# Two transformer blocks in one kernel: in the second expert layer, each expert's down projection is moved behind the next expert's gate and up, and the residual sum and the stores are done per token tile

## The chip, the core and the metric

The kernel runs on 1 core of a Trainium2 chip. The metric is the device time of one execution in microseconds (us), lower is better. Before the change it is 1803.22 us, the median of 3 runs.

The engines are named as the profile names them: PE is TensorE (matmuls; PEld is its weight load), DVE is VectorE, ACT is ScalarE, POOL is GpSimd, SP is SyncE, which here only issues DMAs. SPq is SP's own instruction queue.

## The reference, cut to what matters

Two blocks over 256 tokens of width 1024, all in float32: the first ends in a layer of 32 experts (top 4), the second in a layer of 32 experts (top 2 of one of 4 groups of 8). The change is in the second expert layer, which is the last thing that the program computes:

```python
x = x + mixed @ w_out[l]                                   # residual of the second block
hn = rms_norm_2(x, norm2_w[l]).reshape(B * S, D)
moe = hierarchical_moe(hn, ..., w_gate_experts[l], w_up_experts[l], w_down_experts[l])
x = x + moe.reshape(B, S, D)
```

Each token goes to two experts e. For its row t, an expert computes `silu(t @ w_gate[e]) * (t @ w_up[e])`, of width 512, and multiplies this by `w_down[e]`, back to width 1024. The outputs are weighted by the gates and added up. Each of the three matrices of an expert is 1024 x 512 or 512 x 1024 in float32, 2 MB.

## The kernel before, in words

The tokens lie as two tiles of 128 partitions (TT = 2) in `h`, which holds the residual. `experts(k)` is written once for each engine; k = 0 is the first layer, k = 1 the second. The kernel gives each expert 32 rows (CAP2) in the second layer. Experts with more tokens would be run again from a list afterwards; in these inputs the list is empty.

**The ring.** Weights stream through `ring`, six slots of 2 MB. In the second layer an expert uses three: gate, up and down. Even experts use slots 0 to 2, odd ones slots 3 to 5. SP issues the loads in the order gate, up, down, expert after expert, from one queue. Before each load (L358) it waits for the slot to be free (`free[s]`), and every later load waits behind it. PE raises `free[s]` at the last matmul that reads the slot. I call the loads g0, u0, d0, g1, and so on. The first six (L347) need only slots that the dense part has left; g2 is the first that needs a slot that an expert has left.

**One expert on PE** is made of these steps:

- `gate_up` (L1660): 128 matmuls recorded, 64 for gate, then 64 for up, into bank 4. It waits for `picked` from DVE and for the two loads.
- `gather_rows` of the next expert (L1612): 16 matmuls that pick its rows out of `h`, by the one-hot matrix that DVE's `choose` wrote. ACT copies the rows (L603, `leave_rows`), PE turns them (`turn_rows`, L1621), and DVE's `gather` writes `picked` (L1011).
- `hid_turn` (L1677) turns the hidden values that DVE's `activate` wrote after ACT's sigmoid (L586); ACT copies them (L595, `leave_hid`).
- `down` (L1687): 32 matmuls into bank 5, which wait for that copy. ACT copies the result to `y` (L599, `leave_y`).
- `back_turn` (L1668) turns the gate matrix that DVE's `gate` wrote; ACT copies it (L590, `leave_back`).
- `scatter` (L1715): 16 matmuls that add `y` to the running sum of all experts in banks 0 to 3.

Before the change PE does, for expert p: `gate_up(p)`, `scatter(p-1)`, `back_turn(p)`, `gather_rows(p+1)`, `hid_turn(p)`, `turn_rows(p+1)`, `down(p)`. The down matmuls of an expert so stand ahead of the gate and up matmuls of the next.

**Around the loop.** Banks 0 to 3 are begun by `fill`. Four matmuls of the identity with `h` (L1589, two records each) put the residual into them while DVE chooses the experts, and one more follows behind the rank matmuls (L1595 to L1599). At the end, DVE (L1212) and ACT (L677) copy two column quarters each from banks 0 to 3 into `h`, and SP (L389) issues four stores of 256 KB, one for each quarter.

Of the kernel before, what the change touches and what calls it, by code (L numbers as in the profile page):

```python
# [26 lines left out]
ALU = mybir.AluOpType  # L27
# [29 lines left out]
def two_blocks(nc, w, out):  # L57
# [11 lines left out]
    with ctx:  # L69
# [241 lines left out]
        def _(sp):  # L311
# [74 lines left out]
            rows_out = out[0].rearrange("(a p) n -> p a n", p=P)  # L386
            for b, who, n in ((2, "d2_copied", 17), (0, "moe_out", 5), (3, "d2_copied", 18), (1, "moe_out", 6)):
                sp.wait_ge(sem(who), n)
                sp.dma_start(rows_out[:, :, T * b:T * (b + 1)], h[:, :, T * b:T * (b + 1)]).then_inc(sem("stored"), 16)  # L389
            sp.wait_ge(sem("stored"), 16 * 4)  # L390
# [85 lines left out]
        def _(act):  # L476
# [86 lines left out]
            def experts(k, ready):  # L563
# [84 lines left out]
                else:  # L648
                    def chained(p, n, s0, ahead=True):
                        sigmoid(q, p, n, s0)  # L650
                        leave_back(q, p)
                        if ahead:
                            leave_rows(q, p + 1)
                        leave_hid(q, p)
                        leave_y(q, p, n, s0)

                    chained(0, 0, 0)
                    with act.Fori(0, E // 2 - 1) as n:
                        chained(2 * n + 1, n, 3)
                        chained(2 * n + 2, n + 1, 0)  # L660
                    chained(E - 1, E // 2 - 1, 3, False)
                    after(act, k, q, "pe", "scattered", E - 1)
                act.wait_ge(sem("list"), k + 1)
                n = act.value_load(lst[0:1, 0:1], min_val=0, max_val=NLIST)
                with act.If(n > 0):
                    with act.Fori(0, n) as p:
# [6 lines left out]
                        if k == 1:  # L673
                            after(act, k, q, "pe", "scattered", p)
                if k == 1:
                    for b in range(2, 4):
                        act.copy(h[:, :, T * b:T * (b + 1)], bank(b).rearrange("p (a n) -> p a n", a=TT)).then_inc(sem("d2_copied"), 1)  # L677
# [79 lines left out]
        def _(dve):  # L757
# [167 lines left out]
            def experts(k):  # L925
# [256 lines left out]
                else:  # L1182
                    def chained(p, n, s0, ahead=True):
                        gate(q, p, p, p)
                        if ahead:
                            choose(q, p + 1)
                        activate(q, p, n, s0)
                        if ahead:
                            gather(q, p + 1)

                    chained(0, 0, 0)
                    with dve.Fori(0, E // 2 - 1) as n:
                        chained(2 * n + 1, n, 3)
                        chained(2 * n + 2, n + 1, 0)
                    chained(E - 1, E // 2 - 1, 3, False)
# [14 lines left out]
                if k == 1:  # L1210
                    for b in range(2):
                        dve.tensor_copy(h[:, :, T * b:T * (b + 1)], bank(b).rearrange("p (a n) -> p a n", a=TT))\  # L1212
                            .then_inc(sem("moe_out"), 1)
# [215 lines left out]
        def _(pe):  # L1429
# [133 lines left out]
            def experts(k):  # L1563
# [18 lines left out]
                def fill(n):  # L1582

                    for b in range(n):
                        by_tile = bank(b % 4).rearrange("p (a n) -> p a n", a=TT)
                        if k == 0:
                            pe.matmul(by_tile, nothing[:, 0:P], nothing[:, None, :].broadcast_to([P, TT, T]), start=True, stop=True)
                        else:
                            pe.matmul(by_tile, ident[:, :], h[:, :, T * (b % 4):T * (b % 4 + 1)], start=True, stop=True)  # L1589

                fill((10, 4)[k])
# [140 lines left out]
                fill((2, 1)[k])  # L1732
# [7 lines left out]
                fill((2, 0)[k])  # L1740
                turn_rows(q, 0)
                fill((2, 0)[k])
# [147 lines left out]
                else:  # L1890

                    def chained(p, n, s0, prev, ahead=True):
                        gate_up(q, p, *main(n, s0))
                        if prev is not None:
# [288 lines left out]
```

## Time and profile before

| what | value |
|---|---|
| median of 3 runs | 1803.22 us (1802.41 to 1804.89) |
| the profiled execution, its own time | 1802.41 us |
| its span, first to last instruction | 1800.7 us |
| PE busy, all of the span | 1709.6 us (95%) |
| DVE, ACT busy | 389.8 us (22%), 246.5 us (14%) |
| granted TensorE clock, mean | 0.999 |
| read from HBM | 653.62 MB, 364 GB/s over the span |

How to read it: the profiled execution's own time is 1.7 us above its span, and 0.8 us below the median. The busy shares are means over stages with different limits. The second expert layer is the stretch from about 1340 us to the end. In the chain of work that ended last, PE has 66% of the whole span and DMA 31%; of the latter, the load of `w_up_experts` has 17% of the span and that of the first layer's `w_up` 14%.

### The profile page before, as it was taken

To read this page: it belongs to the slowest core of one execution; us is meant where nothing else is said; L and a number is where in the kernel's file an instruction comes from. 1 tells how busy PE (TensorE), PEld (TensorE's weight loads), DVE (VectorE), ACT (ScalarE), POOL (GpSimd) and SP (SyncE) were. 2 spreads that over 40 slices of the span, in tenths; PEclk is the share of its full clock that TensorE was granted. 3 is DMA by queue.
4 is the path that set the end of the run, shared out by engine and by line. 5 is a ranking of instruction groups with operands and counts; after the bars stand their busy time and mean duration, and the time that the engine had idled before them with its cause. 6 is when DMAs were issued, how large, how long until landed. Compare 5 with 4: busy or idle time off the path is not lost.

```text
span 1800.7 us, 28719 instructions
## 1 busy us (share of the span) xinstructions
PE 1709.6 (95%) x12156; PEld 765.7 (43%) x12156; DVE 389.8 (22%) x943; ACT 246.5 (14%) x529; POOL 28.1 (2%) x107
## 2 busy tenths in 40 slices
PE   8999999999999999999999999999999988888887
PEld 4543333333333333333332335656446655554454
DVE  3542111121212112122121222342331111111111
ACT  2311111111211101001000011130111111111111
POOL 3020000000000000000000000000000000000000
PEclk9999999999999999999999999999999999999999
DMA  9549999999999997999999995431259999999997
GB/s 312 213 164 430 428 428 428 428 429 428 428 429 428 428 427 318 428 428 429 428 428 429 427 401 206 138 119 47 97 227 428 428 429 428 428 429 427 430 428 322
DMA packets 73526, 655.24 MB, mean 364 GB/s; under 512 B 13216, under 2 KB 16048, under 8 KB 36240
## 3 DMA queue, kind: packets, MB, share of 16 engines
q1 hardware_dynamic: 70736, 651.91, 87.1%
q0 software_dynamic: 528, 1.98, 0.4%
q10 hardware_dynamic: 2224, 0.79, 0.2%
q8 instruction: 29, 0.48, 0.1%
q14 instruction: 9, 0.07, 0.0%
HBM read 653.62 MB, written 1.05 MB: 364 GB/s over the span
## 4 chain that ended last, share of the span: by engine, by line
PE 66%; DMA 31%; DVE 1%; ACT 0%; issue 0%; SPq 0%; ACTq 0%; DVEq 0%
PE ps L1627 28%; DMA ring<-in_w_up_experts 17%; DMA ring<-in_w_up 14%; PE ps L1930 6%; PE ps L1660 6%; PE ps L1990 6%; PE ps L1451 3%; PE ps L1612 3%; PE ps L1709 2%; PE ps L1519 2%; PE ps L1636 1%; PE ps L1621 1%; PE ps L1773 1%; PE ps L1675 1%; PE ps L1687 1%; PE ps L2055 1%
## 5 line engine op out<-in xcount | busy, mean ns | idle before, releaser
L1627 PE MATMUL ps<-ring,Z 128*64 128x512 f32 x3072 | 678.2, 595 | 13.4 <-DMA ring<-in_w_up 12.8
L1627 PEld LDWEIGHTS ps<-ring,Z 128*64 128x64 f32 x3072 | 213.6, 137 | 449.6 <-issue 415.1
L1660 PE MATMUL ps<-ring,Z 128*32 128x128 f32 x4096 | 246.4, 408 | 37.4 <-DMA ring<-in_w_up_experts 24.6
L1660 PEld LDWEIGHTS ps<-ring,Z 128*32 128x32 f32 x4096 | 153.1, 126 | 128.3 <-DMA ring<-in_w_up_experts 36.8
L1990 PE MATMUL ps<-ring,xT 128*128 128x512 f32 (+1 forms) x256 | 105.7, 567 | 0.0
L1612 PE MATMUL ps<-h,Z 128*32 128x256 f32 (+1 forms) x776 | 99.8, 468 | 0.3 <-DVE Z L997 0.3
L1027 DVE TENSOR_SCALAR Z<-ps 128x512 f32<-128x512 f32 x32 | 22.1, 692 | 355.8 <-PE ps L1627 355.8
L1039 DVE TENSOR_TENSOR Z<-Z,ps 128x128 f32<-128x128 f32 x32 | 9.2, 288 | 304.6 <-ACT Z L586 304.6
L599 ACT COPY Z<-ps 128x256 f32<-128x256 f32 (+1 forms) x63 | 30.1, 478 | 303.6 <-PE ps L1627 229.6
L1029 DVE TENSOR_SCALAR Z<-ps 128x512 f32<-128x512 f32 x32 | 22.1, 692 | 227.7 <-PE ps L1627 227.7
L1990 PEld LDWEIGHTS ps<-ring,xT 128*128 128x128 f32 x256 | 47.6, 190 | 48.9 <-issue 48.2
L590 ACT COPY Z<-ps 128x256 f32<-128x256 f32 x64 | 23.8, 373 | 317.2 <-PE ps L1668 317.1
L1709 PE MATMUL ps<-Z 64*128 64x512 f32 x256 | 63.6, 615 | 0.8 <-ACT Z L599 0.8
L1687 PE MATMUL ps<-ring,Z 128*32 128x256 f32 x1024 | 61.9, 382 | 0.4 <-ACT Z L595 0.4
L1451 PE MATMUL ps<-ring,xT 128*128 128x512 f32 x128 | 57.3, 606 | 2.7 <-DMA ring<-in_w_in 2.7
L1011 DVE TENSOR_TENSOR Z<-ps,gcol 128x512 f32<-128x512 f32 (+1 forms) x65 | 36.4, 560 | 99.2 <-PE ps L1621 99.1
L1930 PE MATMUL ps<-ring,xT 128*128 128x512 f32 x128 | 56.1, 594 | 1.5 <-DVE xT L1226 0.8
L583 ACT ACTIVATE Z<-Z 128x512 f32<-128x512 f32 x32 | 20.2, 632 | 244.4 <-DVE Z L1027 244.4
L1019 DVE TENSOR_SCALAR Z<-iota,Z 128x128 f32<-128x128 f32 x128 | 38.5, 343 | 42.7 <-issue 41.3
L586 ACT ACTIVATE Z<-ps 128x128 f32<-128x128 f32 x32 | 8.9, 278 | 270.7 <-PE ps L1660 270.7
L1612 PEld LDWEIGHTS ps<-h,Z 128*32 128x32 f32 (+1 forms) x776 | 29.3, 117 | 38.0 <-issue 29.8
L1709 PEld LDWEIGHTS ps<-Z 64*128 64x128 f32 x256 | 22.1, 186 | 41.5 <-issue 41.5
(421 smaller groups left out, 1167.4 us busy)
## 6 DMA issues: line engine op xcount, KB each, us to landing
ring<-in_w_gate SPq DMA_DIRECT2D x64, 2048.0 KB, 18.6
ring<-in_w_up SPq DMA_DIRECT2D x64, 2048.0 KB, 21.6
ring<-in_w_down SPq DMA_DIRECT2D x64, 2048.0 KB, 18.7
ring<-in_w_gate_experts SPq DMA_DIRECT2D x32, 2048.0 KB, 25.3
ring<-in_w_up_experts SPq DMA_DIRECT2D x32, 2048.0 KB, 25.4
ring<-in_w_down_experts SPq DMA_DIRECT2D x32, 2048.0 KB, 24.9
ring<-in_w_in SPq DMA_DIRECT2D x12, 2048.0 KB, 12.4
ring<-in_w_out SPq DMA_DIRECT2D x4, 2048.0 KB, 19.7
```

Of the source, the lines that this page charges most:

```text
L599: act.copy(y[:, 0:(512, 256)[k]], bank((7, 5)[k])[:, 0:(512, 256)[k]]).then_inc(done_by(q, "act", "y"), 1)
L1011: tt(picked[:, 0:DC * CAPS[k]].rearrange("p (c j s) -> p c j s", **by_chunk), bank(6)[:, 0:DC * CAPS[k]].rearrange("p (c j s) -> p c j s", ...
L1019: ts(gated[:, a].rearrange("p (j s) -> p j s", s=CAPS[k]), iota[:, None, 0:CAPS[k]].broadcast_to([P, P // CAPS[k], CAPS[k]]), rank[:, a, d ...
L1451: last = pe.matmul(bank(j % 2), xT[:, c, a * P:(a + 1) * P], slot(u, DC, 512)[:, c, :], start=c == 0, stop=c == DC - 1)
L1519: last = pe.matmul(bank((4, 5, 0, 1)[b]), xT[:, c, a * P:(a + 1) * P], slot(4 + n, DC, 512)[:, c, :], start=c == 4, stop=c == 3)
L1612: last = pe.matmul(bank(6)[n * j:n * (j + 1), 0:P * c].rearrange("p (q c) -> p q c", c=c), one_hot[:, a, 0:n], h[:, a, :].rearrange("p (q ...
L1627: last = pe.matmul(dst[CAP * j:CAP * (j + 1)], lhsT, rhs(j), start=start, stop=True, skip_group_check=True)
L1660: last = pe.matmul(bank(4)[CAP2 * t:CAP2 * (t + 1), P * s:P * (s + 1)], picked[:, chunk * CAP2:(chunk + 1) * CAP2], v[:, c, t:512:4], star ...
L1687: last = pe.matmul(bank(5)[CAP2 * t:CAP2 * (t + 1), 0:T], hid[:, CAP2 * j:CAP2 * (j + 1)], v[:, j, T * t:T * (t + 1)], start=j == 0, stop= ...
L1709: last = pe.matmul(bank(2 * a + j), back[CAP * j:CAP * (j + 1), a * P:(a + 1) * P], y[CAP * j:CAP * (j + 1), :], start=False, stop=True, s ...
L1930: last = pe.matmul(dst, lhs(c), rhs(c), start=c == 0, stop=c == nc_ - 1)
L1990: last = pe.matmul(bank(i % 2)[:, 0:n], tile(a)(c), v[:, c, :], start=c == 0, stop=c == DC - 1)
```

## The change

In the second expert layer (k = 1; the first is left as it is) the loops of PE, ACT and DVE are written anew as `overlapped`:

- PE now does, for expert p: `gate_up(p)`, `gather_rows(p+1)`, `down(p-1)`, `turn_rows(p+1)`, `hid_turn(p)`, `scatter(p-1)`, `back_turn(p)`. `down(E-1)` and `scatter(E-1)` follow behind the loop. ACT and DVE take their steps in the order that goes with this.
- The `ahead` flag is gone: the last expert too gathers and turns rows for a next one. Nothing uses them.
- The residual no longer goes through the fills. `fill` is now matmuls of bfloat16 zeros in both layers, in the second layer 16 ahead of the choice (before: 4 of `h`), then 3, 1 and 1 (before: 1, 0 and 0).
- At the end DVE alone adds banks 0 to 3 to `h`, one instruction of 128 x 1024 for each token tile, and SP stores each tile as one DMA of 512 KB. ACT's two copies are gone.
- ACT's and DVE's waits for `scattered` are changed to fit.

```diff
--- before.py
+++ after.py
@@ -383,11 +383,10 @@
             last_use = [max(x[1] for x in middle[s::SLOTS]) for s in range(SLOTS)]
             experts(1, lambda s: sp.wait_ge(sem("dense2"), last_use[s]))
 
-            rows_out = out[0].rearrange("(a p) n -> p a n", p=P)
-            for b, who, n in ((2, "d2_copied", 17), (0, "moe_out", 5), (3, "d2_copied", 18), (1, "moe_out", 6)):
-                sp.wait_ge(sem(who), n)
-                sp.dma_start(rows_out[:, :, T * b:T * (b + 1)], h[:, :, T * b:T * (b + 1)]).then_inc(sem("stored"), 16)
-            sp.wait_ge(sem("stored"), 16 * 4)
+            for a in range(TT):
+                sp.wait_ge(sem("moe_out"), 4 + a + 1)
+                sp.dma_start(out[0, a * P:(a + 1) * P, :], h[:, a, :]).then_inc(sem("stored"), 16)
+            sp.wait_ge(sem("stored"), 16 * TT)
 
 
         @block.gpsimd
@@ -646,20 +645,20 @@
                     with act.Fori(EXTRA_AT + 1, E) as p:
                         chained(p)
                 else:
-                    def chained(p, n, s0, ahead=True):
+                    def overlapped(p, n, s0, prev=None):
                         sigmoid(q, p, n, s0)
+                        leave_rows(q, p + 1)
+                        if prev:
+                            leave_y(q, *prev)
+                        leave_hid(q, p)
                         leave_back(q, p)
-                        if ahead:
-                            leave_rows(q, p + 1)
-                        leave_hid(q, p)
-                        leave_y(q, p, n, s0)
-
-                    chained(0, 0, 0)
+
+                    overlapped(0, 0, 0)
                     with act.Fori(0, E // 2 - 1) as n:
-                        chained(2 * n + 1, n, 3)
-                        chained(2 * n + 2, n + 1, 0)
-                    chained(E - 1, E // 2 - 1, 3, False)
-                    after(act, k, q, "pe", "scattered", E - 1)
+                        overlapped(2 * n + 1, n, 3, (2 * n, n, 0))
+                        overlapped(2 * n + 2, n + 1, 0, (2 * n + 1, n, 3))
+                    overlapped(E - 1, E // 2 - 1, 3, (E - 2, E // 2 - 1, 0))
+                    leave_y(q, E - 1, E // 2 - 1, 3)
                 act.wait_ge(sem("list"), k + 1)
                 n = act.value_load(lst[0:1, 0:1], min_val=0, max_val=NLIST)
                 with act.If(n > 0):
@@ -670,11 +669,6 @@
                         leave_back(q, p)
                         leave_hid(q, p)
                         leave_y(q, p, p, 0)
-                        if k == 1:
-                            after(act, k, q, "pe", "scattered", p)
-                if k == 1:
-                    for b in range(2, 4):
-                        act.copy(h[:, :, T * b:T * (b + 1)], bank(b).rearrange("p (a n) -> p a n", a=TT)).then_inc(sem("d2_copied"), 1)
 
             experts(0, lambda a: act.wait_ge(sem("residual"), 3 + a))
 
@@ -1180,19 +1174,21 @@
                         chained(p)
                     after(dve, k, q, "dve", "picked", E)
                 else:
-                    def chained(p, n, s0, ahead=True):
+                    def overlapped(p, n, s0):
+                        choose(q, p + 1)
+                        if n is not None:
+                            after(dve, k, q, "pe", "back", p - 1)
                         gate(q, p, p, p)
-                        if ahead:
-                            choose(q, p + 1)
+                        if n is not None:
+                            after(dve, k, q, "pe", "hid", p - 1)
                         activate(q, p, n, s0)
-                        if ahead:
-                            gather(q, p + 1)
-
-                    chained(0, 0, 0)
+                        gather(q, p + 1)
+
+                    overlapped(0, None, 0)
                     with dve.Fori(0, E // 2 - 1) as n:
-                        chained(2 * n + 1, n, 3)
-                        chained(2 * n + 2, n + 1, 0)
-                    chained(E - 1, E // 2 - 1, 3, False)
+                        overlapped(2 * n + 1, n, 3)
+                        overlapped(2 * n + 2, n + 1, 0)
+                    overlapped(E - 1, E // 2 - 1, 3)
                 n = dve.value_load(lst[0:1, 0:1], min_val=0, max_val=NLIST)
                 after(dve, k, q, "pe", "scattered", E - 1)
                 q = f"o{k}_"
@@ -1208,9 +1204,9 @@
                         leave(q, p)
                         after(dve, k, q, "pe", "scattered", p)
                 if k == 1:
-                    for b in range(2):
-                        dve.tensor_copy(h[:, :, T * b:T * (b + 1)], bank(b).rearrange("p (a n) -> p a n", a=TT))\
-                            .then_inc(sem("moe_out"), 1)
+                    for a in range(TT):
+                        row = h[:, a, :].rearrange("p (t n) -> p t n", t=4)
+                        tt(row, ps[:, 0:4, 256 * a:256 * (a + 1)], row, ALU.add).then_inc(sem("moe_out"), 1)
 
             experts(0)
 
@@ -1582,13 +1578,10 @@
                 def fill(n):
 
                     for b in range(n):
-                        by_tile = bank(b % 4).rearrange("p (a n) -> p a n", a=TT)
-                        if k == 0:
-                            pe.matmul(by_tile, nothing[:, 0:P], nothing[:, None, :].broadcast_to([P, TT, T]), start=True, stop=True)
-                        else:
-                            pe.matmul(by_tile, ident[:, :], h[:, :, T * (b % 4):T * (b % 4 + 1)], start=True, stop=True)
-
-                fill((10, 4)[k])
+                        pe.matmul(bank(b % 4).rearrange("p (a n) -> p a n", a=TT), nothing[:, 0:P],
+                                  nothing[:, None, :].broadcast_to([P, TT, T]), start=True, stop=True)
+
+                fill((10, 16)[k])
 
                 pe.wait_ge(sem("chosen"), k + 1)
                 rk = bank(5)[:, 0:64]
@@ -1729,7 +1722,7 @@
                     return s0, filled, lambda s: free[s0 + s]
 
                 q = f"m{k}_"
-                fill((2, 1)[k])
+                fill((2, 3)[k])
                 gather_rows(q, 0)
                 pe.wait_ge(sem("listing_dve"), 2 * k + 1)
                 if k == 0:
@@ -1737,9 +1730,9 @@
                 width = (2, 1)[k]
                 pe.matmul(bank(7)[0:E, 400:400 + width], tri[0:E, 0:E], few[0:E, 17:17 + width], start=True, stop=True)\
                     .then_inc(sem("listing_pe"), 1)
-                fill((2, 0)[k])
+                fill((2, 1)[k])
                 turn_rows(q, 0)
-                fill((2, 0)[k])
+                fill((2, 1)[k])
                 pe.wait_ge(sem("listing_dve"), 2 * k + 2)
                 row = bank(7)[0:1, 410:445]
                 if k == 0:
@@ -1889,24 +1882,26 @@
                     scatter(q, E - 1)
                 else:
 
-                    def chained(p, n, s0, prev, ahead=True):
+                    def overlapped(p, n, s0, prev=None):
                         gate_up(q, p, *main(n, s0))
-                        if prev is not None:
-                            scatter(q, prev)
+                        gather_rows(q, p + 1)
+                        if prev:
+                            down(q, prev[0], *main(*prev[1:]))
+                        turn_rows(q, p + 1)
+                        if prev:
+                            after(pe, k, q, "act", "back", prev[0])
+                        hid_turn(q, p)
+                        if prev:
+                            scatter(q, prev[0])
+                        after(pe, k, q, "act", "hid", p)
                         back_turn(q, p)
-                        if ahead:
-                            gather_rows(q, p + 1)
-                        after(pe, k, q, "act", "back", p)
-                        hid_turn(q, p)
-                        if ahead:
-                            turn_rows(q, p + 1)
-                        down(q, p, *main(n, s0))
-
-                    chained(0, 0, 0, None)
+
+                    overlapped(0, 0, 0)
                     with pe.Fori(0, E // 2 - 1) as n:
-                        chained(2 * n + 1, n, 3, 2 * n)
-                        chained(2 * n + 2, n + 1, 0, 2 * n + 1)
-                    chained(E - 1, E // 2 - 1, 3, E - 2, False)
+                        overlapped(2 * n + 1, n, 3, (2 * n, n, 0))
+                        overlapped(2 * n + 2, n + 1, 0, (2 * n + 1, n, 3))
+                    overlapped(E - 1, E // 2 - 1, 3, (E - 2, E // 2 - 1, 0))
+                    down(q, E - 1, *main(E // 2 - 1, 3))
                     scatter(q, E - 1)
                 pe.wait_ge(sem("list"), k + 1)
                 n = pe.value_load(lst[0:1, 0:1], min_val=0, max_val=NLIST)
```

## Rows read from the trace of the kernel before

**Rows 1.** The page's slices: GB/s moved in each fortieth of the span.
```profile
GB/s 312 213 164 430 428 428 428 428 429 428 428 429 428 428 427 318 428 428 429 428 428 429 427 401 206 138 119 47 97 227 428 428 429 428 428 429 427 430 428 322
```

**Rows 2.** Windows: us, busy time of the engines, PEclk, DMA share, GB/s.
```profile
1346.00:1348.00 2.00, 2.00 (x37) 1.15 (x28) 0.00 (x0) 0.00 (x0) 0.00 (x0) 1.00 0.64 246
...
1362.00:1758.00 396.00, 355.13 (x5482) 207.79 (x5478) 54.70 (x194) 43.15 (x138) 0.00 (x0) 1.00 1.01 428
```

**Rows 3.** Timeline of SP's queue, loads g2, u2, d2 and u31 (start us, us).
```profile
1344.62 0.35 SPq L358 DMA_DIRECT2D ring<-in_w_gate_experts  x1
1348.13 0.34 SPq L358 DMA_DIRECT2D ring<-in_w_up_experts  x1
1352.43 0.33 SPq L358 DMA_DIRECT2D ring<-in_w_down_experts  x1
...
1758.81 0.33 SPq L358 DMA_DIRECT2D ring<-in_w_up_experts  x1
```

**Rows 4.** DMA issues: g2, u2, d2, one window each (last number: us to landing).
```profile
ring<-in_w_gate_experts SPq DMA_DIRECT2D x1, 2048.0 KB, 7.7
...
ring<-in_w_up_experts SPq DMA_DIRECT2D x1, 2048.0 KB, 10.0
...
ring<-in_w_down_experts SPq DMA_DIRECT2D x1, 2048.0 KB, 10.5
```

**Rows 5.** Chain that ended last, experts 0 and 1 (start us, us, what).
```profile
1348.45 1.10 PE ps L1612 x16
...
1349.57 0.38 ACT Z L603
...
1349.99 0.51 PE ps L1621 x2
1350.50 1.86 PE ps L1687 x32
1352.37 7.46 PE ps L1660 x113
```

**Rows 6.** Chain that ended last, from the landing of u31 to the last scatter.
```profile
1784.25 3.87 PE ps L1660 x61
1788.12 1.08 PE ps L1715 x16
1789.20 0.38 PE ps L1668 x2
...
1790.03 0.34 PE ps L1677
...
1790.40 0.27 ACT Z L595
...
1790.71 1.98 PE ps L1687 x32
...
1793.23 1.18 PE ps L1715 x16
```

**Rows 7.** Timeline of the last microseconds, and the landing of the last two stores.
```profile
1794.65 1.29 DVE L1212 COPY h<-ps 128x512 f32<-128x512 f32 x2 [5.54 <-PE ps L1715]
...
1795.78 2.01 SPq L389 DMA_DIRECT2D out<-h  x4
...
out<-h SPq DMA_DIRECT2D x2, 256.0 KB, 2.9
```

**Rows 8.** Groups by line and form: a DVE sum of 1024 columns (busy us, mean ns).
```profile
L850 DVE TENSOR_TENSOR Z<-Z,st 128x1024 f32<-128x1024 f32 x2 | 2.5, 1226 | 0.1
```

**Rows 9.** Timeline: fill of zeros (first layer); fills, rank matmuls and first gather (second layer).
```profile
116.26 2.32 PE L1587 MATMUL ps<-zeros 128*128 128x512 bf16 x10
...
1331.09 3.68 PE L1589 MATMUL ps<-h,ident 128*128 128x512 f32 x8
...
1335.56 0.41 PE L1595 MATMUL ps<-Z,tri 128*128 128x32 f32 x2 [0.78 <-DVE Z L974]
...
1337.71 0.61 PEld L1612 LDWEIGHTS ps<-h,Z 128*32 128x32 f32 x16 [0.86 <-DVE Z L997]
```

## The prediction

> **What bounds the kernel now.** I read the page's slices first, since the change touches only the last 460 us. In them the DMA rate stands at 427 to 430 GB/s in nearly every slice of the last quarter [rows 1]. Then the windows: from 1362 to 1758 us the DMA engines move 428 GB/s without a break, while PE is busy for 355 of 396 us [rows 2]. So the stream of weights is the bound of this stage, and PE has about 10% to spare. One load is 2.097 MB, which at 428 GB/s is 4.90 us; an expert has three, 14.7 us, of which PE works 0.90 x 14.7 = 13.2 us.
>
> The timeline of SP's queue and the time to landing confirm the pace: d2 was issued at 1352.43 and took 10.5 us, so it landed at 1362.93 [rows 3, 4]. PE took up u31 at 1784.25 [rows 6]. Between them lie 86 loads (g3 to u31): 421.3 / 86 = 4.90 us. What the reader is to see is that any microsecond in which the stream stands still during this stage is lost for good: there is no later gap that could take it up. PE's speed matters in two places only: at the start, where PE's releases of slots start the stream again, and behind the last load.
>
> The start shows such a standstill already. The first six loads had filled the ring; g2 could be issued only at 1344.62, when PE had left slot 0, and in the two us before 1348 the rate is still 246 GB/s [rows 2, 3]. u2 and d2 followed 3.5 and 7.8 us later, both in time: with g2 and u2 in the queue there are 9.8 us of work.
>
> **The change, part by part.**
>
> *Start of the stage: 0.* A fill of zeros costs 0.22 us when many follow each other (10 in 2.32 us from start to end, of which the last one's own length is a part) [rows 9]. Sixteen take 3.5 us. The four fills of `h` begin at 1331.09 and take 3.68 us, and then the rank matmuls wait 0.78 us for DVE, to 1335.56; that is 4.5 us. So the sixteen are covered; without that cover they would cost up to 3.5 us. Behind the ranks 3 x 0.22 replace one fill of `h`, but the first gather's weight load waits 0.86 us for DVE's one-hot, so nothing is won. The last two fills lie in waits for ACT and DVE and cost nothing; uncovered, 0.4 us.
>
> *Where d2's slot comes free: +7.2 us.* This is the main term. Slot 2 is freed by `down(0)`. Before, it stood ahead of `gate_up(1)` and d2 was issued at 1352.43. Now PE must first do gate_up(1). From the chain: gather of expert 1 begins at 1348.45, behind a back_turn of 0.38 which now comes later, so gate_up(0) ends at 1348.07. Then gather 1.10, ACT's copy with its two handovers 0.44, turn_rows 0.51 [rows 5], hid_turn 0.34, ACT's copy 0.27 with handovers 0.33, back_turn 0.38 [rows 6], gate_up(1) 7.46, gather of expert 2 1.10, down(0) 1.86 [rows 5]. The sum is 13.52, so d2 is issued at 1361.6, 9.2 us later than before. Loads g3 and u3, whose slots are free by then, wait behind it on SP. The queue holds only g2 and u2 when d2 is late: 16.98 us between the issues of g2 and d2, of which these two fill 2 x 4.90. The stream stands for 16.98 - 9.80 = 7.2 us.
>
> A second way: d2 meets an empty queue as g2 did, so it lands 7.7 us after its issue, and the load behind it lands 5.8 us later (g2 at 1352.32, u2 at 1358.13) instead of 4.9 [rows 3, 4]. That is d2 at 1369.3 against 1362.9, 6.4 later, and g3 7.3 later. I keep 6.4 as the lower bound and take 8.0 as the upper one (7.3, and another 0.7 for handovers of PE).
>
> Here a page's rule speaks otherwise. The rows show 428 GB/s for hundreds of us [rows 2]. The Trainium skill, "DMA: Bandwidth & Descriptors", section "Where 436 GB/s comes from", says that for HBM to SBUF the side of HBM binds at about 358 GB/s. By it a load would take 5.86 us and the stall would be 16.98 - 11.7 = 5.3 us, an estimate from that page; the trace disagrees, and the sum goes by the trace.
>
> *Later releases: 0.* In the steady state, with u(p) landing at T, PE ends gate_up(p) at T + 3.9 and down(p-1) at T + 6.9. The load that needs this slot starts to flow at T + 14.7. So it is issued some 8 us ahead. PE's own work per expert falls slightly, and all of it lies in time in which PE would wait for the stream; the extra waits removed are worth nothing.
>
> *Behind the last load: +2.5 us.* Before, from the end of gate_up(31) at 1788.12 to the end of the last scatter at 1794.41 it is 6.3 us: scatter 1.08, back_turn 0.38, two copies and hid_turn, down 1.98, y's copy, scatter 1.18 [rows 6]. Now there follow: gather of a 33rd expert 1.10, down(30) 1.86, turn_rows 0.51, hid_turn about 0.2 (its result is not waited for at once), scatter(30) 1.08 (it covers ACT's copy of hid), back_turn 0.38, down(31) 1.98, ACT's copy of y 0.38 with handovers 0.16, scatter 1.18: 8.8 us. d31 lands 4.9 us behind u31 and so ahead of its use. Bounds: 2.3 and 2.9.
>
> *The end: +0.1 us.* Before, DVE began 0.24 us behind the last scatter, the fourth store was issued 2.9 us behind it (1795.78 + 2.01 - 0.5 - 1794.41) and took 2.9 us to land [rows 7]. Now two DVE sums of 1024 columns take 2 x 1.23 [rows 8], so the second store is issued at 0.24 + 2.46 = 2.7 us. It has twice the bytes, 0.6 us more at 428 GB/s, but only one store ahead of it. Bounds of its landing: 2.9 (nothing for the bytes) and 3.5; I take 3.2. That gives 5.9 against 5.8. Bounds for the end: -0.2 and +0.6, the latter with a slower read of four banks by DVE.
>
> Sum: 0 + 7.2 + 2.5 + 0.1 = +9.8 us. The profiled execution took 1802.41, so 1812.2; the median is 0.8 above it: 1813.0 us.
>
> **The rivals.**
>
> *A, the stall is absorbed.* Before, loads later come 25 us ahead of their use (u31 is issued at 1758.81 and taken at 1784.25) [rows 3, 6], which looks like slack. Were it so, only the tail would be left: 1803.2 + 2.6 = 1805.8, no change that can be told. Against it: those 25 us are time in the queue, not slack of the stream, which never falls below its rate [rows 1, 2].
>
> *B, faster.* The new order takes ACT's copy out of PE's path (0.44 us for each expert in [rows 5]). If PE set the pace, 31 x 0.44 = 13.6 us would go and 2.6 come: 1792.2. This decides only if the three loads took less than PE's 13.2 us, which is 477 GB/s; the rows show 428.
>
> *C, a second stall or a slower stream.* d3 waits for down(1): 1361.6, then 0.51 + 0.34 + 1.08 + 0.38, gate_up(2) 7.46, gather and down 2.96 make 1374.3. u3 lands at about 1380.0, and its flow ends up to 2.8 us earlier (7.7 - 4.9); d3 needs up to 2.8 us from issue to flow. So the margin lies between 0.1 and 2.9 us. A PE late by 3 us would cost up to 3 us more; from d4 on the margin grows by 1.5 us or more for each expert. The same price comes from a stream that is 1% slower because fewer loads stand in it (4.2 us). Speaking against the latter: with 10 us to landing, the rate was full already [rows 2, 4]. Time: about 1816.5.
>
> **How the numbers follow.** Forecast 0.79, C 0.12, A 0.06, B 0.03. A measurement of this kernel can tell about 0.2%, 3.6 us, from no change. Forecast and C are slower by more: 0.91; A is within: 0.06; B is faster: 0.03. The bounds of the forecast alone are 6.4 + 2.3 - 0.2 = 8.5 and 8.0 + 2.9 + 0.6 = 11.5, so 1811.7 to 1814.7; the runs before spread by 2.5 us. With part of C, and room below for a PE that reaches down(0) earlier, the range is 1809.5 to 1817.0.
>
> **What would show it.** The changed profile should show d2 issued about 17 us behind g2, a landing of about 7.7 us for it, a window near 1356 to 1363 us with hardly any GB/s, 428 GB/s from there on, u31 taken up near 1791.5, the last scatter about 12.7 us behind that (10.2 before), and two stores. The prediction is wrong if d2 is issued before about 1354.5, if the stream stands again at d3, or if any stretch runs well above 428 GB/s.

## The result, and the profile after

The changed kernel takes 1816.0 us (median of 4 runs, 1814.09 to 1817.25) against 1803.28 us: a ratio of 1.0064, 95% interval 1.0052 to 1.0077. A second comparison, of a plain copy of it on another occasion, gave 1814.45 against 1805.36, 1.0049 (1.0035 to 1.0063). So it is slower by 9 to 13 us; 1813.0 was forecast. The profiled execution took 1813.94 us, with a span of 1812.1.

The timeline of SP's queue shows the main term. These are the loads g1 (L347) and g2, u2, d2, g3, u3, d3 (start us, us); the rows of before are [rows 3].

```profile
1328.39 0.33 SPq L347 DMA_DIRECT2D ring<-in_w_gate_experts  x1
...
1346.91 0.35 SPq L358 DMA_DIRECT2D ring<-in_w_gate_experts  x1
1350.42 0.34 SPq L358 DMA_DIRECT2D ring<-in_w_up_experts  x1
1363.38 0.33 SPq L358 DMA_DIRECT2D ring<-in_w_down_experts  x1
1363.91 0.33 SPq L358 DMA_DIRECT2D ring<-in_w_gate_experts  x1
1364.34 0.38 SPq L358 DMA_DIRECT2D ring<-in_w_up_experts  x1
1375.63 0.33 SPq L358 DMA_DIRECT2D ring<-in_w_down_experts  x1
```

d2 comes 16.5 us behind g2, where before it came 7.8 us behind, and g3 and u3 stand right behind d2, half a microsecond apart: they had been free to go and waited for it in the queue. The windows of the changed kernel (the columns of [rows 2]; the last three are PEclk, DMA share and GB/s) show what the stream did in the meantime:

```profile
1356.00:1358.00 2.00, 2.00 (x44) 1.35 (x36) 0.00 (x0) 0.00 (x0) 0.00 (x0) 1.00 1.03 442
1358.00:1360.00 2.00, 2.00 (x42) 1.40 (x38) 0.00 (x0) 0.00 (x0) 0.00 (x0) 1.00 0.22 90
1360.00:1362.00 2.00, 2.00 (x40) 1.42 (x36) 0.57 (x2) 0.61 (x2) 0.00 (x0) 1.00 0.00 0
1362.00:1364.00 2.00, 1.96 (x33) 1.15 (x24) 0.20 (x1) 0.50 (x3) 0.00 (x0) 1.00 0.00 0
1364.00:1366.00 2.00, 2.00 (x30) 1.30 (x34) 1.06 (x5) 0.54 (x2) 0.00 (x0) 1.00 0.93 213
1374.00:1760.00 386.00, 327.80 (x5194) 200.95 (x5189) 55.15 (x187) 44.43 (x134) 0.00 (x0) 1.00 1.01 429
```

From 1358 to 1366 us little or nothing moves, 6.7 us' worth of transfers in all, and PE is busy all the while, which is why PE's row shows no harm; then the old rate without a break. PE is now busy for 85% of that long stretch instead of 90%: the new order does make PE's loop shorter, and the time is spent in waiting for weights.

The chain that ended last, from the landing of u31 (start us, us, what; before: [rows 6]):

```profile
1793.29 3.88 PE ps L1653 x59
1797.17 0.93 PE ps L1605 x15
1798.10 1.73 PE ps L1680 x32
1799.82 0.43 PE ps L1614 x2
1800.26 0.11 PE ps L1670
...
1800.43 1.15 PE ps L1708 x16
1801.57 0.37 PE ps L1661 x2
1801.94 1.91 PE ps L1680 x32
...
1803.87 0.38 ACT Z L598
...
1804.39 1.18 PE ps L1708 x16
```

Behind the up half (L1653) stand the gather for a 33rd expert (L1605), down(30) (L1680), that expert's turn_rows (L1614), and only then what was there before. From 1797.17 to 1805.57 it is 8.4 us, where it was 6.3.

At the start of the stage something shows that was not forecast. The windows of the changed kernel around the first gather:

```profile
1338.00:1340.00 2.00, 1.67 (x19) 0.72 (x22) 1.82 (x13) 0.00 (x0) 0.00 (x0) 0.88 1.01 434
1340.00:1342.00 2.00, 2.00 (x18) 0.83 (x10) 0.99 (x8) 0.93 (x2) 0.00 (x0) 0.50 1.04 442
1342.00:1344.00 2.00, 2.00 (x32) 1.05 (x34) 1.62 (x10) 0.72 (x1) 0.00 (x0) 0.77 1.01 434
```

and the chain there:

```profile
1339.25 1.75 PE ps L1605 x16
1341.00 0.19 PE ps L1731 x2
1341.19 0.54 PE ps L1581
1341.73 0.45 PE ps L1614 x2
1342.18 0.43 PE ps L1581
```

The granted clock falls to 0.50, which is 1.2 GHz instead of 2.4. The first gather takes 1.75 us instead of 1.10, and a fill of zeros 0.54 and 0.43 instead of 0.22, and both of the last fills are now in the chain. Ahead of it, PE had run 16 fills of zeros and 3 more, with two waits for DVE between; before, fills of `h` stood there, and the clock was 1.00 throughout.

To compare executions I cut each one at four points: the issue of g1, the issue of g2, the landing of u31, the end of PE's last scatter, and the end of the span. All lengths are in us, from the timelines of SP and PE, the time to landing and the span:

| kernel | g1 at | g1 to g2 | g2 to u31 landed | to last scatter | to end of span | g1 to end |
|---|---|---|---|---|---|---|
| before | 1326.9 | 17.8 | 439.6 | 10.2 | 6.3 | 473.8 |
| changed | 1328.4 | 18.5 | 446.3 | 12.3 | 6.6 | 483.7 |
| difference | 1.5 | 0.8 | 6.7 | 2.1 | 0.3 | 9.9 |

The 1.5 us ahead of g1 lie in parts of the program that the change leaves as they were. The experiments below show g1 anywhere between 1325.7 and 1331.5.

### The profile page after: what moved, and what is told of

It reads as the page before. It is cut to its first block, busy times and chain, and to the rows that moved or that the text cites. A ratio compares the mean times of both kernels' runs of the same rounds, so it can differ in the third digit from the quotient of the medians.

```text
span 1812.1 us, 28778 instructions
## 1 busy us (share of the span) xinstructions
PE 1701.0 (94%) x12185; PEld 772.9 (43%) x12185; DVE 394.8 (22%) x946; ACT 248.5 (14%) x528; POOL 28.0 (2%) x107
## 4 chain that ended last, share of the span: by engine, by line
PE 63%; DMA 34%; DVE 2%; SPq 1%; issue 1%; ACT 0%; DVEq 0%
PE ps L1620 26%; DMA ring<-in_w_up_experts 18%; DMA ring<-in_w_up 15%; PE ps L1925 6%; PE ps L1985 6%; PE ps L1653 4%; PE ps L1447 3%; PE ps L1605 3%; PE ps L1702 2%; PE ps L1680 2%; PE ps L1515 2%; PE ps L1629 1%; PE ps L1614 1%; PE ps L1766 1%; PE ps L1668 1%; SPq L358 1%
## 5 line engine op out<-in xcount | busy, mean ns | idle before, releaser
L1653 PE MATMUL ps<-ring,Z 128*32 128x128 f32 x4096 | 246.7, 408 | 62.7 <-DMA ring<-in_w_gate_experts 33.1
L1653 PEld LDWEIGHTS ps<-ring,Z 128*32 128x32 f32 x4096 | 147.5, 126 | 152.9 <-DMA ring<-in_w_up_experts 44.3
L1605 PE MATMUL ps<-h,Z 128*32 128x256 f32 (+1 forms) x792 | 102.0, 470 | 0.7 <-DVE Z L991 0.7
L1680 PE MATMUL ps<-ring,Z 128*32 128x256 f32 x1024 | 61.5, 379 | 0.0
L1605 PEld LDWEIGHTS ps<-h,Z 128*32 128x32 f32 (+1 forms) x792 | 36.0, 125 | 36.7 <-issue 24.8
L1680 PEld LDWEIGHTS ps<-ring,Z 128*32 128x32 f32 x1024 | 36.4, 109 | 19.7 <-issue 0.2
```

The lines of the kernel that those rows point to most:

```text
L1605: last = pe.matmul(bank(6)[n * j:n * (j + 1), 0:P * c].rearrange("p (q c) -> p q c", c=c), one_hot[:, a, 0:n], h[:, a, :].rearrange("p (q ...
L1653: last = pe.matmul(bank(4)[CAP2 * t:CAP2 * (t + 1), P * s:P * (s + 1)], picked[:, chunk * CAP2:(chunk + 1) * CAP2], v[:, c, t:512:4], star ...
L1680: last = pe.matmul(bank(5)[CAP2 * t:CAP2 * (t + 1), 0:T], hid[:, CAP2 * j:CAP2 * (j + 1)], v[:, j, T * t:T * (t + 1)], start=j == 0, stop= ...
```

## The experiments

Each kernel has a profile and is timed in 5 rounds against the kernel before. Two copies of one kernel make the yardstick, so they come first.

**Both kernels once more, unchanged.**

> The kernel before once more, unchanged, as a measure of what two copies of one kernel differ by: the ratio should hold 1 within 0.1%. By the traces so far, the first expert layer and the dense part end up to 5 us apart from one execution to the next (g1 issued from 1325.7 to 1330.9 us); if that is scatter, this copy's g1 lies in the same band, and g1 to the last scatter takes 467.5 us within 0.5.

> The changed kernel once more, beside the other copies on one chip. Its g1 to the last scatter should take 477.2 us within 0.5, 9.6 above before; the median 9.5 to 11 us above that of before here. If instead the difference is 12 us or more with the same 9.6 us in this stage, something outside the stage is slower with the change.

Measured: the copy of before 1804.55 us against 1805.36, ratio 0.9995 (0.9986 to 1.0005), g1 at 1329.7 and g1 to the end of the span 473.7, within 0.2 us of its first profile though g1 came 2.9 us later. The copy of the changed kernel 1814.45 us, ratio 1.0049 (1.0035 to 1.0063), g1 at 1330.7 and g1 to the end 483.8; g1 to the last scatter 477.3 against 467.4. So the lengths from g1 on repeat within 0.2 us, and the 10 us by which the two kernels differ there lie in this stage. What lies ahead of g1 scatters by some us. In all five profiles with g1 at 1330.6 or later the granted clock is 0.66 or 0.83 between 1150 and 1160 us, and in four of them 0.66 to 0.83 between 290 and 300 us too; in none of the other nine.

**One part of the change at a time: the order alone.** The loops as in the changed kernel; fills, final sum and stores as before:

```diff
-                fill((10, 16)[k])          # and zeros in both layers
+                fill((10, 4)[k])           # k == 1: ident x h
-                        tt(row, ps[:, 0:4, 256 * a:256 * (a + 1)], row, ALU.add)
+                        dve.tensor_copy(h[:, :, T * b:T * (b + 1)], bank(b)...)   # and ACT's two, four stores
```

> The new order of the loops alone; the fills of h, the four column quarters and their stores are as before. Theory 1 (the stream of weights stands still while d2 waits for down(0) behind gate_up(1), and the path behind the last load is longer): the span from the issue of g2 to the landing of u31 grows by 6.7 us against before (439.6), the path from u31 to the last scatter by 2.1 us (10.2 before), and the stage starts as before, since the fills of h are back: 8.8 us in all, about 1812.1. Theory 2 (the residual part and the clock that falls to 0.5 at the start of the stage cause much of the loss): the order alone costs clearly less, 1808 or below. Where this run comes out near 1816, neither the residual part nor the clock has a share.

**The residual part alone.** The reverse of these edits, in the kernel before.

> The residual part alone (fills of zeros, sum and stores per token tile); the loops keep the order of before. Theory 1: the clock falls at the start of the stage as in the changed kernel, 0.8 us, and the end is 0.2 us longer: 1.0 us, about 1804.3. Theory 2: it costs 3 to 5 us, since the 1.5 us that the changed kernel was late before this stage, and its wider scatter, come with it too: 1806 to 1808.

Measured: the order alone 1816.32 us against 1805.39, ratio 1.0059 (1.0045 to 1.0072), so 10.9 us where I had expected 8.8. The residual part alone 1805.71, ratio 1.0006 (0.9997 to 1.0015), which excludes the 3 to 5 us of theory 2 and can't tell 1.0 us from none. Lengths:

| kernel | g1 at | g1 to g2 | g2 to u31 landed | to last scatter | to end of span | g1 to end |
|---|---|---|---|---|---|---|
| order only | 1329.5 | 17.8 | 446.7 | 12.2 | 8.1 | 484.8 |
| residual only | 1327.0 | 18.3 | 439.4 | 10.2 | 7.9 | 475.7 |

The stall and the longer path belong to the order, with nothing from the residual part. The late g2 belongs to the residual part; its windows show the clock at 0.59 and 0.56:

```profile
1338.00:1340.00 2.00, 2.00 (x20) 0.74 (x13) 1.23 (x11) 0.57 (x2) 0.00 (x0) 0.59 1.05 451
1340.00:1342.00 2.00, 2.00 (x26) 1.15 (x29) 1.64 (x8) 1.08 (x1) 0.00 (x0) 0.56 0.97 418
```

The end is 1.8 us longer than before in the first and 1.6 in the second, which neither part can account for, since each of them has the stores of one of the two kernels. With the 1.8 us, and a g2 to u31 that is 0.4 us longer than in the changed kernel, the order alone comes to 10.9 us in its profile too. SP's own waits name it. First before, then the order alone:

```profile
SPq L69 <- DMA out<-h: 2.5, 1, 2.5
```

```profile
SPq L69 <- DMA out<-h: 4.1, 1, 4.1
```

The same four stores are waited for 2.5 us in one and 4.1 in the other. With two stores it is 3.2 (changed) or 4.5 (residual only). It is long (3.8 to 4.5) in 7 of the 14 profiles of this study, with either way of storing, and short (2.4 to 3.2) in both profiles of both kernels. What chooses it is open.

**The suspected stall by itself.** Nothing on PE, ACT or DVE is changed; SP waits longer once:

```diff
+                if k == 1:
+                    for u in range(2):
+                        for s, dst, src in expert_loads(1, 2 + u, 3 * u):
+                            if s == 2:
+                                sp.wait_ge(free[4], 1 + FREE0[1][4])
...
```

> The kernel before, all engines' work unchanged; SP alone waits longer once: it issues d2 only when PE has ended gate_up(1) (the release of u1's slot), as if slot 2 came free that late. This is the suspected stall by itself. Theory 1: d2 is issued 15.3 us behind g2 instead of 7.8; g2 and u2 fill 9.8 of it, so the stream stands still for 5.5 us, and all of it is found again at the end: g2 to the landing of u31 445.1 us instead of 439.6, the path behind it 10.2 as before, the time 5 to 5.5 us above before. Theory 2 (loads later run 25 us ahead of their use, so a stall at the start is absorbed): no change.

Measured: 1810.72 us against 1805.36, ratio 1.0034 (1.0024 to 1.0044). d2 is issued 15.4 us behind g2; g2 to the landing of u31 takes 445.2 us, 5.7 more than before; the path behind it 10.1. The windows:

```profile
1358.00:1360.00 2.00, 2.00 (x44) 1.24 (x36) 0.00 (x0) 0.00 (x0) 0.00 (x0) 1.00 0.02 8
1360.00:1362.00 2.00, 2.00 (x40) 1.19 (x36) 0.12 (x1) 0.28 (x1) 0.00 (x0) 1.00 0.00 0
1362.00:1364.00 2.00, 2.00 (x31) 0.86 (x23) 0.45 (x2) 0.37 (x1) 0.00 (x0) 1.00 0.82 172
```

One late issue, 30 experts ahead of the end, is found again in full at the end. Rival A has fallen: later loads are queued 25 us ahead here too, and absorb nothing.

**Where the new order may begin.** In two kernels the first experts keep the old order, 1 in the first and 4 in the second, on all three engines:

```diff
-                    overlapped(0, 0, 0)
+                    chained(0, 0, 0, None)
+                    overlapped(1, 0, 3, (0, 0, 0), False)     # down(0) is done; scatter(0) is not
```

> The changed kernel, but expert 0 runs in the old order: down(0) stands ahead of gate_up(1), and the new order starts with expert 1. Theory 1: d2 is issued 7.8 us behind g2 as before; the late slot is now that of down(1), and d3 is issued near 28 us behind g2 instead of 20.6, of which the stream had some 5 us in hand, so it stands still for about 3 us instead of 6.7. The time falls by 3.7 us against the changed kernel. Theory 2 (not the first late slot, but the new order in every expert costs time): no change against the changed kernel but for noise.

> As the run before, but experts 0 to 3 run in the old order. Theory 1: by then the loads are issued 7 us and more ahead of their need, PE gaining about 2 us for each expert; d6 is late by 9.2 us against before and still in time (or short by under 1 us). g2 to the landing of u31 takes 439.6 to 440.5 us as before, and only the path behind the last load (2.1 us) and the residual part (1.0 us) are left: about 6.7 us below the changed kernel. Theory 2: no change against the changed kernel.

Measured: with expert 0 in the old order 1813.25 us, ratio 1.0042 (1.0028 to 1.0056); with experts 0 to 3, 1809.67, ratio 1.0023 (1.0013 to 1.0034), both against 1805.39. With one old expert d2 is in time and d3 is late, and the stream stands there:

```profile
1374.00:1376.00 2.00, 2.00 (x41) 1.58 (x36) 0.57 (x2) 0.63 (x2) 0.00 (x0) 1.00 0.42 172
1376.00:1378.00 2.00, 1.97 (x33) 1.25 (x24) 0.21 (x1) 0.50 (x3) 0.00 (x0) 1.00 0.00 0
1378.00:1380.00 2.00, 2.00 (x30) 1.29 (x34) 1.02 (x5) 0.53 (x2) 0.00 (x0) 1.00 0.92 229
```

In four of the kernels the loss follows one rule within 0.3 us: the distance from g2 to the late load, less 4.90 us for each load queued between. In the two with the switch at 4 (the second of them is the next experiment) it doesn't.

| kernel | late load | behind g2 | loads between | rule gives | g2 to u31, more than before |
|---|---|---|---|---|---|
| changed | d2 | 16.5 | 2 | 6.7 | 6.7 |
| order only | d2 | 16.6 | 2 | 6.8 | 7.1 |
| d2 late | d2 | 15.4 | 2 | 5.6 | 5.7 |
| switch at 1 | d3 | 28.8 | 5 | 4.3 | 4.6 |
| switch at 4 | d6 | 67.1 | 14 | below 0 | 1.7 |
| switch at 4 and back | d6 | 67.2 | 14 | below 0 | 1.6 |

My 3 us for the switch at 1 had a wrong figure for what the stream had in hand. With the switch at 4 d6 should be in time with 1.5 us to spare (67.1 less 14 x 4.90), and yet 1.7 us are lost. These are u6 and d6 there, first their issues and then their times to landing:

```profile
1397.69 0.33 SPq L358 DMA_DIRECT2D ring<-in_w_up_experts  x1
1411.29 0.33 SPq L358 DMA_DIRECT2D ring<-in_w_down_experts  x1
...
ring<-in_w_up_experts SPq DMA_DIRECT2D x1, 2048.0 KB, 19.3
...
ring<-in_w_down_experts SPq DMA_DIRECT2D x1, 2048.0 KB, 12.1
```

From d3 to u6 every load lands within 0.2 us of before, counted from the issue of g2. Then d6 lands 6.4 us behind u6 instead of 4.9, and every load behind it stays 1.7 us late. So this loss too is at the load whose slot comes late. It is no standstill: no window of 2 us stands out, and in the 100 us behind g2 the stream moves 420 GB/s against 421, a quarter of a microsecond's worth. Why d6 lands so much later than that was not tried.

**Back to the old order for the last expert.** The switch at 4, and down(30) ahead of gate_up(31), nothing gathered for a 33rd:

```diff
-                    overlapped(E - 1, E // 2 - 1, 3, (E - 2, E // 2 - 1, 0))
-                    down(q, E - 1, *main(E // 2 - 1, 3))
+                    down(q, E - 2, *main(E // 2 - 1, 0))
+                    chained(E - 1, E // 2 - 1, 3, E - 2, False)
```

> The changed kernel with experts 0 to 3 in the old order, and expert 31 too: down(30) stands ahead of gate_up(31), and no rows are gathered for a 33rd expert. Theory 1 (two places cost: the late slot at the start and the path behind the last load): the path from the landing of u31 to the last scatter is 10.2 us again instead of 12.3, g2 to the landing of u31 is 441 us as in the run before with the switch at 4; experts 4 to 30 in the new order cost nothing. So 2.1 us below the switch at 4, and within 3 us of the kernel before. Theory 2 (the new order costs something in every expert): 27 experts in the new order keep most of the loss, and the time stays 4 us or more above before.

Measured: 1807.12 us against 1805.46, ratio 1.0010 (1.0001 to 1.0019). The path behind u31 is 10.1 us again. From g2 to the landing of u31 it is 441.2 us, 1.6 more than before, and again d6 lands 6.4 us behind u6; behind d6 the distance to before stays the same within 0.1 us. So the new order costs 1.6 us where it is taken up, with the first late slot, and nothing from there to expert 30. With 0.6 us from the clock at the start and 0.9 at the stores its profile is 3.2 us longer than before from g1 on; the medians differ by 1.7.

**The tail alone**, in the kernel before, with the loads in the old order:

```diff
-                    chained(E - 1, E // 2 - 1, 3, E - 2, False)
+                    gate_up(q, E - 1, *main(E // 2 - 1, 3))
+                    down(q, E - 2, *main(E // 2 - 1, 0))
+                    hid_turn(q, E - 1)
+                    scatter(q, E - 2)
...
+                    back_turn(q, E - 1)
+                    down(q, E - 1, *main(E // 2 - 1, 3))
```

> The kernel before, in which only down(30) is moved behind gate_up(31), with the old order of loads; no rows are gathered for a 33rd expert. Theory 1: the stream is untouched (g2 to the landing of u31 439.6), and behind the landing of u31 stand gate_up's up half 3.9, down(30) 1.8, hid_turn 0.2, scatter 1.1, back_turn 0.4, down(31) 1.9, ACT's copy 0.5, scatter 1.2: 11.0 us instead of 10.2. So 0.8 of the changed kernel's 2.1 us is the order, and 1.3 the gather and turn of a 33rd expert's rows. Its time is 0.8 us above before, which the median can't tell from none.

Measured: the path from u31 to the last scatter is 11.3 us. The 0.3 us over my figure is ACT's copy of y(30), which without the 33rd expert's turn is no longer hidden: in the chain, `ACT Z L599` takes 0.38 us between down(30) and scatter(30). So of the 2.1 us, 1.1 is the order; the rest, 1.0, I put down to the 33rd expert. The time is 1809.39 against 1805.36, 1.0021 (1.0011 to 1.0030). That is 4 us, not 0.8. Its profile shows 1.6 up to the last scatter, of which 0.5 is a late landing of g30 that nothing in the edit explains, and 1.7 at the stores; the rest is not explained.

**The same order of work, with another order of loads.** In the changed kernel, SP issues g(p+1) and u(p+1) ahead of d(p):

```diff
+                    load(2, 1, (0, 1))
+                    load(3, 1, (0, 1))
+                    load(2, 1, (2,))
+                    with sp.Fori(2, E // 2) as n:
+                        load((n * 2, 0), n, (0, 1))
+                        load((n * 2 - 1, 3), n - 1, (2,))
+                        load((n * 2 + 1, 3), n, (0, 1))
+                        load((n * 2, 0), n, (2,))
+                    load(E - 1, E // 2 - 1, (2,))
```

> The changed kernel, only the order of the loads on SP is another: from expert 2 on, gate and up of the next expert are issued ahead of down of this one (g2, u2, g3, u3, d2, g4, u4, d3, ..., g31, u31, d30, d31). Theory 1 (the slot of d2 comes late, and SP's queue makes g3 and u3 wait behind it): g3 is issued about 10.2 us behind g2, the stream stands still for 0.4 us instead of 6.7, and the last data to come is now a down matrix, of which less work hangs: the last scatter ends some 3.7 us behind the last landing. 9 to 10 us below the changed kernel, level with before or 1 us under it. Theory 2 (the new order of PE's work is slower by itself, whatever the loads do): at most 3 us below the changed kernel.

Measured: 1806.97 us against 1805.46, ratio 1.0011 (1.0002 to 1.0020), where the changed kernel had 1.0064 and its copy 1.0049. g1 to the last scatter is 468.1 us: 9.1 less than in the changed kernel, 0.6 more than before, and as much as the clock costs at the start (g1 to g2 18.4 instead of 17.8). The stores are waited for 4.4 us here instead of 2.5, which also lies in the 1.5 us between the medians. g3 is issued 10.3 us behind g2, and d2 as late as ever, 16.6 us, with nothing behind it that it holds up. PE's work and its order are the same, so it is the queue that makes the late slot expensive. At the end, the chain shows that only down, a copy and a scatter hang on the last landing, 3.8 us:

```profile
1775.89 17.44 DMA ring<-in_w_down_experts
...
1793.46 1.97 PE ps L1700 x32
...
1795.45 0.38 ACT Z L618
...
1795.97 1.18 PE ps L1728 x16
```

**Two tries for a version that beats both.** Both start from the kernel before and load g2 and u2 as two halves each, released by PE half by half in gate_up(0). The first also puts the last expert's back_turn between its gate and up matmuls; the second also uses the new order and the new load order for the last pair.

```diff
+                    for s, dst, src in expert_loads(1, 2, 0)[0:2]:
+                        sp.wait_ge(sem("x_pe"), len(X_PE) + s + 1)
+                        sp.dma_start(dst[:, 0:2048], src[:, 0:2048])...
+                        sp.wait_ge(free[s], 1 + FREE0[1][s])
+                        sp.dma_start(dst[:, 2048:4096], src[:, 2048:4096]).then_inc(full[s], 16)
...
```

> The kernel before, with two edits at its two ends: g2 and u2 are loaded as two halves each, and PE releases slots 0 and 1 half by half in gate_up(0), so that the stream starts again 1.95 us earlier; and the last expert's back_turn stands between its gate and up matmuls (with a buffer of its own), so that ACT's copy and back_turn leave the path behind the last load (0.84 us). If the stage is bound by the stream from the first release on and by the path behind the last load, 2.8 us come off the kernel before: g1 to the landing of u31 1.9 shorter, u31 to the last scatter 9.4 instead of 10.2. If the restart is bound by something else (d2, or the landing of halves), the first gain is missing or smaller.

> The kernel before with the halves of the run before, and the new order for the last pair alone: g31 and u31 are loaded ahead of d30, and down(30) stands behind gate_up(31). The last data to land is d31, and only down, ACT's copy and a scatter hang on it: the last scatter ends 3.6 us behind the landing of d31, where before it is 5.3 us (u31 lands 4.9 us ahead of d31, 10.2 us ahead of the last scatter). So 1.6 us come off at the end and 1.9 at the start: 3.5 us below before. If the order costs by itself wherever it stands, the end is not shorter.

Measured: 1806.06 us, 1.0005 (0.9996 to 1.0014), and 1806.98, 1.0010 (1.0001 to 1.0019), both against 1805.46. Neither beats before. In the first the tail came as worked out: 9.4 us from u31 to the last scatter instead of 10.2, which leaves g1 to the last scatter 0.8 us shorter than before. In the second the last scatter ends 3.8 us behind the landing of d31 instead of 5.3, but d31 lands 1.1 us later than before, so g1 to the last scatter is 467.1 (before 467.5). The halves didn't bring the later landings forward. The first half of g2 was issued 2.0 us earlier as meant, but g1 to the landing of u31 is 457.3, as before within 0.1. In the first kernel, the windows behind that issue (1346.59):

```profile
1347.00:1349.00 2.00, 2.00 (x40) 1.42 (x36) 0.00 (x0) 0.00 (x0) 0.00 (x0) 1.00 0.72 188
1349.00:1351.00 2.00, 2.00 (x43) 1.61 (x37) 0.00 (x0) 0.00 (x0) 0.00 (x0) 1.00 1.00 320
1351.00:1353.00 2.00, 2.00 (x34) 1.12 (x30) 0.45 (x2) 0.65 (x2) 0.00 (x0) 1.00 0.79 258
```

Six us at 60% of the rate. In the 40 us behind g1 the stream moved 385 GB/s against 379 before, half a microsecond's worth more, and yet from g4 on every load landed as before within 0.2 us; why was not tried. And both kernels have the long wait for the stores, 1.7 to 2.0 us, which is more than the tails gained.

## Why the prediction was right, point by point

- **The bound** was read rightly: the stream of weights, with PE some 10% below it. The run with d2 late alone shows it most plainly: 5.6 us of standing still by the rule, 5.7 us at the end.
- **Start of the stage: 0** was wrong, it is +0.8 us. The times of the fills held (16 in 3.62 us), and they are covered as I said. What I left out is the clock: with fills of zeros it fell at this place in 6 of 7 profiles (g1 to g2 18.3 to 18.6 us), with fills of `h` in none of 7 (17.6 to 17.8 where g2 is loaded whole).
- **d2's slot: +7.2 us** measured +6.7. d2 came 16.5 us behind g2 instead of 17.0: gathers and downs that run into other work take 0.93 and 1.77 us in the chain instead of 1.10 and 1.86, and hid_turn 0.12 instead of 0.34. Its landing took 8.8 us, not 7.7, and g3 landed 13.5 us behind its issue; the difference of issues was the better of my two ways.
- **The 358 GB/s of the Trainium skill** ("DMA: Bandwidth & Descriptors", "Where 436 GB/s comes from") would have made the stall 5.3 us, by the estimate in the prediction; the rate was 429 again over 386 us, and 6.7 us came out.
- **Later releases: 0** held in the changed kernel: from 1374 us on the rate is 429, and every load from g4 to u31 lands 6.7 or 6.8 us later than before, counted from g2. The margin is narrower than the rule says: with the switch at 4 a d6 that the rule has in time still lost 1.5 us.
- **Behind the last load: +2.5 us** measured +2.1, 8.4 us for 8.8, from the same shorter pieces. 1.1 is the order, the rest the 33rd expert.
- **The end: +0.1 us** measured +0.3. The sums take 1.23 us each, and a store of 512 KB landed in 3.1 us (median of the two) for 3.2 taken.
- **The sum, +9.8 us**, meets 9.9 us from g1 on. That it meets so closely is partly luck: the stall and the tail came 0.9 us short, the clock and the end 1.0 us over. The 12.7 us between the first medians hold some 3 us more, of which the two profiles show 1.5 ahead of g1, in parts that scatter; the copy's 1814.45 against 1805.36 is 9.1.
- **Rivals.** A fell with the late d2. B fell: PE is busy for 85% instead of 90%, and the time grew. C did not come: d3 was issued 28.7 us behind g2, 2.5 us earlier than the rule asks (5 loads of 4.90 and the stall of 6.7 make 31.2), and landed 4.9 us behind u3 as the rate has it.

## What to carry to other kernels

When a stream of weights is the bound, write the releases of the slots beside the order of the loads, and take the distance between two issues less the transfers queued between them: what is left over was lost for good in every kernel here. Leave a margin too: here a load that the rule had in time by 2.5 us cost nothing, and one with 1.5 us to spare cost 1.5. A step moved later on the compute engine delays its slot's release; if its load stands in an in-order queue ahead of loads that could go, change the order of the loads with it. Then look at what hangs on the last load, for there the loop's steady state, in which the order is free, has ended.

## What the runs showed of the hardware that I had not expected

- The granted clock of TensorE fell from 2.4 to 1.2 GHz for about 3.4 us (from the windows above) after 3.6 us of fills of bfloat16 zeros and two waits for DVE; it did so in six of seven profiles, and with float32 products of `h` in their place in none of seven. Whether the zeros, the type or the length of the waits decides was not tried. In the first layer of the kernel before, ten such fills and more of them behind the ranks left the clock at 1.00. The clock fell in places that no edit touches as well, near 11 us in six of the fourteen profiles, so chance may have a part in it.
- A load of 1 MB into an empty queue landed after 6.5 and 6.8 us. One of 2 MB (g2) landed after 7.5 to 7.9 us in eleven profiles and 8.7 in one; d2 into the empty queue, with g3 and u3 issued right behind it, after 8.7 to 9.1.
- A load's landing can move otherwise than the bytes of the stream: with the switch at 4, landings from d6 on were 1.7 us late with a quarter of a microsecond of bytes missing, and with g2 and u2 in halves half a microsecond of bytes was gained and from g4 on no landing came earlier by more than 0.2 us.
- The same stores at the end are waited for 2.5 or 4.1 us, by kernel and not by their form, as far as one or two profiles of each can say.
